# First pass of grouped-query scores on 64 rows, two heads at a time into two banks; shifts turned by DMA

## What is computed

```python
def attend(q, k, v):
    B, Lq, H, hd = q.shape
    kvh = k.shape[2]
    qg = q.reshape(B, Lq, kvh, H // kvh, hd)
    s = jnp.einsum('bqkgd,bskd->bkgqs', qg, k).astype(jnp.float32) * ATTN_SCALE
    p = jax.nn.softmax(s, axis=-1).astype(v.dtype)
    o = jnp.einsum('bkgqs,bskd->bqkgd', p, v)
    return o.reshape(B, Lq, H * hd)
```

## Time and profile before

| what | value |
|---|---|
| median of 3 executions | 1237.08 us (1236.64 to 1238.64) |
| the profiled execution | 1236.43 us, of which its span is 1234.6 us |
| busy share of the span | TensorE 99%, VectorE 79%, ScalarE 51%, GpSimd 32% |
| granted TensorE clock | 0.999 of full speed |
| windowed attention | about 290 to 365 us |
| grouped-query steps | about 365 to 536 us |

### The profile page before, as it was taken

How to read it: one execution, slowest core, us unless ns; L and a number is a source line. 1 busy time by engine, 2 the same in 40 slices (tenths; PEclk the granted TensorE clock), 3 DMA queues, 4 the chain that set the end, 5 groups by cost and what they waited for, 6 DMA issues and landing times.

```text
span 1234.6 us, 22333 instructions
## 1 busy us (share of the span) xinstructions
PE 1216.6 (99%) x7901; PEld 657.4 (53%) x7901; DVE 978.9 (79%) x1597; ACT 632.7 (51%) x1203; POOL 398.6 (32%) x385
## 2 busy tenths in 40 slices
PE   8999999999999999999999999999999999999998
PEld 1564655556666666664454545555554554444444
DVE  4779999767879999954489888888888875767587
ACT  2542224447779999943155455445545543412324
POOL 0000000115778988830320543445554420000001
PEclk9999999999999999999999999999999999999999
DMA  9728645665310131021300333232223317997953
GB/s 363 279 81 328 246 122 105 177 127 148 112 44 11 35 138 36 2 104 41 113 35 7 97 104 102 85 93 79 74 79 100 102 51 269 348 347 242 370 188 137
DMA packets 135681, 170.35 MB, mean 138 GB/s; under 512 B 33200, under 2 KB 94640, under 8 KB 134192
## 3 DMA queue, kind: packets, MB, share of 16 engines
q1 hardware_dynamic: 135600, 169.28, 41.9%
HBM read 138.57 MB, written 22.55 MB: 130 GB/s over the span
## 4 chain that ended last, share of the span: by engine, by line
PE 79%; DVE 11%; ACT 3%; DMA 3%; issue 2%; POOL 1%; SPq 0%; POOLq 0%; DVEq 0%; ACTq 0%
PE PS L1392 76%; DMA arena<-in_x 1%; PE PS L1721 1%; DVE arena L2784 1%; DMA arena<-weight_sum_rows 1%; PE PS L1467 1%; DVE arena L3509 1%; DVE arena L2640 1%; DVE arena L3512 1%; ACT arena L2594 1%; ACT PS L2324 1%; DVE arena L3072 0%; POOL arena L1236 0%; DVE arena L2978 0%; DVE arena L2896 0%
## 5 line engine op out<-in xcount | busy, mean ns | idle before, releaser
L1392 PE MATMUL PS<-arena 128*128 128x512 f16 (+9 forms) x7485 | 1184.1, 319 | 11.4 <-DMA arena<-in_w_mod 4.2
L1392 PEld LDWEIGHTS PS<-arena 128*128 128x128 f16 (+3 forms) x7485 | 617.0, 100 | 557.8 <-issue 37.4
L3188 DVE SCALAR_TENSOR_TENSOR arena<-arena 128x512 f16<-128x512 f32 x128 | 112.2, 883 | 30.3 <-ACT arena L2416 29.6
L2416 ACT ACTIVATE arena<-arena 128x512 f16<-128x512 f32 x120 | 75.4, 631 | 102.4 <-PE PS L1392 102.4
L2546 ACT ACTIVATE arena<-arena 128x512 f16<-128x512 f32 x77 | 48.1, 629 | 124.2 <-DVE arena L3409 72.1
L3072 DVE TENSOR_REDUCE arena<-PS 128x1 f32<-128x512 f32 (+1 forms) x160 | 106.7, 679 | 2.6 <-PE PS L1392 2.6
L1252 POOL TENSOR_TENSOR arena<-arena 128x2 f32<-128x2 f32 (+1 forms) x18 | 20.5, 1137 | 217.0 <-DVE arena L2925 217.0
L1386 POOL TENSOR_TENSOR arena<-arena 128x1 f32<-128x1 f32 x8 | 4.7, 596 | 231.5 <-DVE arena L3576 227.2
L2319 ACT ACTIVATE arena<-PS 128x512 f16<-128x512 f32 x125 | 75.1, 601 | 2.6 <-PE PS L1392 1.5
L1236 POOL TENSOR_TENSOR arena<-arena 128x512 f16<-128x512 f32 x64 | 74.0, 1157 | 6.9 <-ACT arena L2324 4.3
L3245 DVE TENSOR_TENSOR arena<-PS,arena 128x256 f32<-128x256 f32 (+1 forms) x100 | 55.2, 553 | 25.7 <-PE PS L1392 25.4
(11 more groups left out here) (224 smaller groups left out, 1231.1 us busy)
## 6 DMA issues: line engine op xcount, KB each, us to landing
arena<-in_w_ffn_out SPq DMA_DIRECT2D x121, 256.0 KB, 5.0
arena<-in_w_mod SPq DMA_DIRECT2D x23, 1024.0 KB, 7.1
arena<-in_w_ffn_in SPq DMA_DIRECT2D x88, 256.0 KB, 3.0
left_operands<-arena SPq DMA_DIRECT2D x43, 256.0 KB, 3.0
arena<-in_w_in SPq DMA_DIRECT2D x9, 1024.0 KB, 5.8
arena<-left_operands SPq DMA_DIRECT2D x3, 2816.0 KB, 12.6
arena<-lay_bias SPq DMA_DIRECT2D x12, 512.0 KB, 4.1
arena<-in_x SPq DMA_DIRECT2D x2, 2048.0 KB, 14.6
```

The lines of the kernel that those rows point to most:

```text
L1392: return pe.matmul(out, lhsT, rhs, start=start, stop=stop, skip_group_check=True)
L2416: act.activation(block_split(p, b)[:, 0], weight_block(p, b, first), ACT.Copy, scale=WS).then_inc(blk_hi, 1)
L3188: dve.scalar_tensor_tensor(dst[:, 1], src, WS, dst[:, 0], ALU.mult, ALU.subtract).then_inc(blk_lo, 1)
```

## The change

The queries are stacked differently: an odd head now has its low part in rows 0 to 63 and its high part in rows 64 to 127. The first pass then multiplies the high parts alone, on 64 rows: an even head on rows 0 to 63, an odd one on rows 64 to 127. In the steps two such chunks make a pair: their products stand next to each other in TensorE's list and write banks 4 and 5, and one reduction of 1024 elements a partition gives both maxima. A pair is issued every second step, up to 15 steps ahead; in steps 0 to 3 there is one in each. A pair waits until the pair before is reduced. Twelve chunks (before 11) are made singly among the units, ten of them on 64 rows. The steps' four banks are 0, 2, 1, 3, and the first pair also waits until the last query tile has left bank 4.

The shifts are no longer turned by TensorE and copied by ScalarE and GpSimd. The stacked queries of each tile are stored to DRAM after their transposing DMA; SyncE loads the high queries of a group into the shifts' tile (two tiles now), and when the maxima are there a transposing DMA turns the whole tile into `q2`. The loads of weights and rows that SyncE issues later in the stage are spread among the groups, and TensorE waits for the landing (`q2_in`) ahead of the second product of a group. The turn for group 1 no longer waits for the last query tile. On GpSimd one low part of the output weights moves behind `low_p2`. The added bound in the shift is doubled, since the low parts of the queries are left out of the maximum.

```diff
-LEAD, LAG, SHIFT_AT, SEND_AT = 13, 4, 8, 4
-CATCH_UP = (3, 6)
+EARLY_CHUNKS = NKT + 2
+FIRST_PAIRS = {n: EARLY_CHUNKS // 2 + n for n in range(4)}
+LEAD, LAG, SEND_AT = 15, 4, 4
-CHUNK_BANK, STEP_BANK, OUT_BANK = (5, 1), (0, 2, 4, 3), (6, 7)
+CHUNK_BANK, STEP_BANK, OUT_BANK = 4, (0, 2, 1, 3), (6, 7)
...
+            def load_high_queries(g):
+                t, kv = divmod(g, HKV)
+                sp.wait_ge(q_out[t % 2], q_out_from[t % 2] + 16 * (t // 2 + 1))
...
+                for r in range(2):
+                    sp.dma_start(shifts[kv][:, r:GROUP:2, 0:HD], halves[:, :, 3 * r]).then_inc(qh_in, 16)
+
+            def turn_shifts(g):
+                t, kv = divmod(g, HKV)
+                sp.wait_ge(qh_in, 32 * (g + 1))
+                sp.wait_ge(sh_rdy, g + 1)
...
+                sp.dma_start_transpose(q2_by_head, shifts[kv].rearrange("p h d -> p (h d)")).then_inc(q2_in, 16)
...
             def chunk(c):
...
+                    ins = mm(ps, qT[own_rows(h), GROUP * c.kv + h, tok(c.t)], k[own_rows(h), o:o + 512], True, True)
...
+            def pair(c):
+                if c.s == EARLY_CHUNKS:
+                    pe.wait_ge(pr_n, n_normed(NU - 1))
                     for u in (NU - 3, NU - 2):
                         pe.wait_ge(*qk_turned(u))
+                pe.wait_ge(s_max, n_chunked(c.ahead(-1)))
...
+                for h, a, b in blocks:
+                    for r in range(2):
+                        rows = own_rows(r)
+                        ins = mm(PS[:, CHUNK_BANK + r, a:b], qT[rows, GROUP * c.kv + h + r, tok(c.t)],
+                                 k[rows, o:o + b - a], True, True)
                 ins.then_inc(s_mm, 1)
-
-            def turn_shifts(s):
-                pe.wait_ge(sh_rdy, s.g + 1)
...
-                if s.s == NKT:
-                    pe.wait_ge(*qk_turned(NU - 1))
-                for h in range(GROUP):
-                    ins = mm(PS[:, shift_bank(s), h * P:h * P + P], shifts[:, h * P:h * P + P], ident16, True, True)
-                ins.then_inc(sh_mm, 1)
...
                 if s.i == 0:
-                    pe.wait_ge(q2_hi, s.g + 1)
-                    pe.wait_ge(q2_lo, s.g + 1)
+                    pe.wait_ge(q2_in, 16 * s.g + 16)
...
             def step(s):
                 step_scores(s)
-                for c in s.chunks():
-                    chunk(c)
-                if s.turns_shifts():
-                    turn_shifts(s.ahead(NKT - s.i))
+                for c in s.pairs():
+                    pair(c)
                 if s.s >= LAG:
                     step_weigh(s.ahead(-LAG))
...
-            def copy_shifts(s):
-                act.wait_ge(sh_mm, s.g + 1)
-                act.copy(q2[s.kv][HD:P], PS[HD:P, shift_bank(s)]).then_inc(q2_lo, 1)
...
+            def pair_maximum(c):
...
+                both = PS[:, CHUNK_BANK:CHUNK_BANK + 2]
                 if c.i < 2 * GROUP:
+                    h = c.chunk_head()
+                    ins = dve.tensor_reduce(mx[:, c.kv, h:h + 2, c.i // 2 % 2], both, AX, ALU.max)
...
+                ins.then_inc(s_max, 1)
+                if c.i == NKT - 2:
+                    query_shifts(c)
...
-            for s in range(1, BODY):
-                step(Step(s))
-            for s in range(BODY, NSTEPS):
+            for s in range(NSTEPS):
                 step(Step(s))
```

## The result

The changed kernel takes 1242.18 us (median of 6 runs, 1241.02 to 1243.24) against 1237.2 us of the kernel before (6 runs): 1.0038 of it, 95% interval 1.0025 to 1.0051. It is 5.0 us slower, where 2.7 were forecast. The profiled execution is one of the longer ones (1242.9 us, span 1241.1), and that of before (1236.43, span 1234.6) was shorter than all six runs of before, so the two traces lie 6.5 us apart, and 1.5 of that is scatter between executions.

The account below looks back on a forecast made before the run. TensorE was taken to bound windowed attention, with TensorE, VectorE or ScalarE setting the pace along the grouped-query steps. +2.0 + 3.3 - 2.6 = +2.7 us on 1236.43 gave 1239.1, as a median 1239.8 us; range 1232.5 to 1246, the forecast's own 1237 to 1243.

Parts of the forecast that it names:

- A pair at 0.42: Groups: two 64-row products side by side take 0.42 us of TensorE with the drains, against 0.43 for two chunks before.
- Rival A: Groups and units: the drain costs nothing, a pair takes 0.24, VectorE sets the groups; about 1232.8 us; chance 0.18.
- Term 1: Units of windowed attention: ten single chunks on 64 rows each pay two changes of row form on TensorE; +2.0 us.
- Term 2: Seam, first scores to step 10: first pair waits for bank 4, later pairs for the maximum before; +3.3 us.
- a rival's second case: Seam: TensorE's idle stretches of 3.0 and 2.7 us bring the clock to 1.2 GHz; 1242 to 1243; rival's whole chance 0.17.
- Term 3: Groups: TensorE loses the turn, one stall for a maximum of about 0.25; a group takes 10.26; -2.6 us together.
- the 3.4 taken: Groups: the median landing time, in us, of transposing DMAs of this width (2.4 to 5.4), leaving 1.6 to spare.
- the 0.50 for VectorE's scaling: Groups that scale output weights: the scaling adds 0.50 us to VectorE's work, 9.51 without it, 10.01 with it.
- Rival B's first case: Groups: the turning DMA lands at 5.4 or later each time, 15 groups lose 0.4 to 1; 1246 to 1255; whole rival 0.17.
- Its third case: Groups: float16 row groups don't run side by side, a pair takes 0.63, 13 groups lose 1 us each; 1253; whole rival 0.17.
- Rival C: Seam: waits for bank 4 and the end of unit 31 overlap more, costing 1 us instead of 3.3; 1237.5; chance 0.10.

Follow-up runs that it names:

- the first experiment: Changed kernel plus 20 products nobody reads, put where TensorE waits at the seam (eight, nine and three ahead of the first three pairs): 1240.23 us, 1.0029.
- GpSimd's old steps: GpSimd takes the low parts of steps 1, 4, 6 and 8, as in the changed kernel: 1242.18 us, and 1241.85 us, 1.0036, when run once more.
- the queues moved: Changed kernel with weight loads behind the turns of groups 4, 8, 12 on SyncE's queue and VectorE's weight scaling in step 8, not 0: 1240.07 us, 1.0026.
- GpSimd's new steps: Changed kernel with GpSimd taking the low parts of steps 1, 3, 6 and 8 instead of 1, 4, 6 and 8: 1238.56 us, 1.0013.
- the last 2.2 us: Changed kernel with early chunks on 128 rows, first pair behind unit 31's turn, queues and GpSimd's steps moved: 1234.63 us, 0.9982, 2.2 us under the kernel before.

## Why the prediction was right, and where not

- **A pair at 0.42, with 0.09 empty on either side** (term 3's first number): right; 0.416 in the records, 0.095 ahead of the pair. The drain that was read from float32 products of another stage holds for these. Rival A needed a pair under 0.35 and is out.
- **Term 1, +2.0:** right, 0.20 for each of ten units, and gone with the chunks on 128 rows.
- **Term 2, +3.3:** right in its list, up to 0.2 at each step to the third pair, and 3.2 with the clock held. What was put apart as a rival's second case, the clock's fall at the idle stretches of about 3 us, came as well, in all six profiles with that order and no added products. In the five of them with pairs on 64 rows it cost 0.6 to 1.8 and not the 2.2 to 3.2 that I gave it, as TensorE was not the one that all waited for. The step that failed is the division into cases: the fall of the clock does not exclude the forecast, it adds to it, and should have stood in the sum with a chance.
- **Term 3, -2.6:** the model of a group was right (10.26 forecast, 10.24 measured wherever nothing else came in, with the one stall of 0.25 where it was expected), but the gain in the first profile was 0.8. Two steps of it failed. "SyncE's new waits hold back its later loads, whose users come groups later" looked at that queue from one side: the loads also hold back the turns behind them, and slow them in flight. Groups 4 and 12 lost 0.47 each to this in the first profile, though a turn lands in 2.5 at the median, sooner than the 3.4 taken. And the 0.50 for VectorE's scaling is no constant: beside GpSimd's instructions it took up to 0.83, and in four groups this cost TensorE 0.2 (the last section has the rows' rule); groups whose scaling took 0.62 or 0.63 lost nothing, and in the profile of the first experiment 0.76 to 0.78 cost some 0.14. Together 1.7 in the first profile, and 0.9 to 2.1 in the four others with pairs on 64 rows, the old queue and GpSimd's old steps; with the queues moved, groups 1 to 13 fell to 133.1 us, 2.1 under before, and with the 0.56 measured in the last two groups that is the -2.6.
- **Rival B's first case** (every turn late) did not come: two turns of fifteen were waited for in the first profile, and for those both the queue and a landing of 4.35 and 4.83 were to blame. **Its third case**, products that don't run side by side, is refuted by the two starts 0.003 apart. **Rival C** asked for step 10 less than 16 us after the first scores; it came at 18.4.

So the sign and the parts that follow from the rows held; the 2.3 us between 2.7 and 5.0 are 1 to 2 in the groups and about 1 of clock. Closer than that the sum can't be drawn, as both differ from execution to execution. That 1242.18 still lies in the forecast's own range of 1237 to 1243 is owed to the width of that range: term 3 had less than a third of its gain.

Not tried: the turns by DMA alone in the kernel before, and the one maximum alone; what each of them is worth by itself stays open. GpSimd's new steps were not tried in the kernel before either, so not all of the last 2.2 us need come from the change.

## What to carry to other kernels

Two half-height products side by side between full-height ones save next to no time of the array when each change of form costs 0.095 us; what they gave here is that both results are ready 0.11 earlier, which counts only where somebody waits for them. A half-height product that stands alone pays for the two changes of form and gains nothing. When work is moved to a DMA queue, read the queue in both directions: what the new waits hold back, and what stands (and waits) ahead of the new transfers or moves beside them. And when a stage's first instruction waits for the last of the stage before, put it behind what else is ready in that engine's list: here that one line was worth 2 us.

## What the runs showed of the hardware

- The length of VectorE's scaling of 128x512 float32 depends on GpSimd. It took 0.41 to 0.96, and in twelve of the fourteen traces each of the eight ended 0.28 after the end of the GpSimd instruction that ran at its start; in the two others that instruction ended within 0.1 of the start and the scaling took its shortest, 0.41 to 0.42. The 0.58 in the earlier trace rows is such a wait too. The Trainium skill, "SBUF — State Buffer", section "Who interferes with whom", says that a VectorE instruction in a two-port mode, which `tensor_scalar` can take, contends with GpSimd for a shared pair of ports, and that the first to issue has the pair for its whole length while the other is blocked. These rows agree: a start 0.60 into an instruction of 1.16 us gave 0.83, one 0.40 into one of 0.61 gave 0.49; which mode the scaling took no run shows. VectorE's maxima of 1024 elements kept to 1.21 to 1.23 throughout.
- The granted clock of the same program differs from execution to execution. In the changed kernel, behind idle stretches of TensorE of 2.76, 2.11 and 0.79 us, it was at 0.50 from 377.97 to 381.30 in one profile; in another it was at 0.50 from 370.1 on, inside the first of these stretches, to 373.4, and again from 376.9 to 380.2. Behind stretches of 1.16, 0.42, 1.19 and 0.79 it stayed at 1.00 in three profiles and fell to 0.51 for 3.3 us in a fourth.
- ScalarE's wait near 291 us, for a signal of TensorE that is raised 0.66 to 2.25 us after the modelled end of the product, was 0.58 to 2.17 over 14 profiles. That is a good part of what one profile and the next differ by, so a difference of 1 us between two traces is to be placed before it is explained.
